# Neighbourhood attention cut into units of 16 grid columns by 8 rows with 32 key columns each, and values with both halves of V in one stationary operand

## The reference, cut to what matters

```
col_start = np.clip(qc - NA_WIN_COLS // 2, 0, GRID_W - NA_WIN_COLS)
col_mask = (qc[None, :] >= col_start[:, None]) & (qc[None, :] < col_start[:, None] + NA_WIN_COLS)
...
s_band = jnp.einsum('bqhd,brkhd->bhqrk', q_row, kb).astype(f32) * scale + bias.astype(f32)
s_band = jnp.where(col_mask, s_band, -jnp.inf)
s_ctx = jnp.einsum('bqhd,bchd->bhqc', q_row, k_c).astype(f32) * scale
s = jnp.concatenate([s_band.reshape(B, NA_HEADS, GRID_W, wr * GRID_W), s_ctx], axis=-1)
p = jax.nn.softmax(s, axis=-1).astype(v_c.dtype)
...
return (jnp.einsum('bhqrk,brkhd->bqhd', p_band, vb)
        + jnp.einsum('bhqc,bchd->bqhd', p_ctx, v_c))
```

## Time and profile before

| | us |
|---|---|
| median of 3 runs | 2733.66 |
| lowest, highest | 2729.28, 2734.5 |
| span of the profiled execution | 2731.3 |

### The profile page before, as it was taken

The page is one execution under the profiler, slowest core; times in us unless marked ns, Lnnn a source line. Parts: engine busy times, 40 slices in busy tenths (PEclk is TensorE's granted clock), DMA queues, the critical chain, the costliest instruction groups (busy, mean ns, idle before and its releaser), DMA issues.

```text
span 2731.3 us, 36972 instructions
## 1 busy us (share of the span) xinstructions
PE 2561.5 (94%) x14795; PEld 2194.1 (80%) x14795; DVE 1530.0 (56%) x2878; ACT 1096.8 (40%) x1928; POOL 321.7 (12%) x199
## 2 busy tenths in 40 slices
PE   7988889999997999998799999999899999899998
PEld 6877777878887877776688888889788887788887
DVE  3565556757757677777746443445555555633334
ACT  5455534222234655555521212113555565522223
POOL 2122100000012222221100000002222322000001
PEclk9999999999998999999899999999999999999999
DMA  4111033545531111111133333331322222132331
GB/s 112 47 47 47 24 96 124 166 139 166 166 116 47 32 39 39 39 33 45 48 105 122 103 118 105 116 113 46 72 54 59 62 61 60 62 106 79 105 98 61
DMA packets 247333, 223.86 MB, mean 82 GB/s; under 512 B 36916, under 2 KB 215898, under 8 KB 247162
## 3 DMA queue, kind: packets, MB, share of 16 engines
q1 hardware_dynamic: 247162, 221.49, 27.0%
HBM read 219.24 MB, written 2.22 MB: 81 GB/s over the span
## 4 chain that ended last, share of the span: by engine, by line
PE 78%; DVE 11%; ACT 7%; issue 4%; POOL 0%; DMA 0%; SPq 0%; DVEq 0%; POOLq 0%; ACTq 0%
PE ps L363 24%; PE ps L364 23%; PE ps L365 22%; DVE FR L527 2%; PE ps L2820 1%; PE ps L652 1%; ACT FR L522 1%; ACT whi L388 1%; PE ps L1071 1%; PE ps L2406 1%; ACT FA L2499 1%; PE ps L2831 1%; DVE hT L2579 1%; DVE FA L2619 1%; DVE raw L1444 1%
## 5 line engine op out<-in xcount | busy, mean ns | idle before, releaser
L363 PE MATMUL ps<-Uh,whi 128*128 128x512 f32 (+2 forms) x2544 | 904.8, 356 | 24.1 <-ACT FA L2518 5.9
L364 PE MATMUL ps<-Ul,whi 128*128 128x512 f32 (+2 forms) x2544 | 889.2, 350 | 0.0
L365 PE MATMUL ps<-Uh,wlo 128*128 128x512 f32 (+2 forms) x2544 | 887.7, 349 | 0.0
L363 PEld LDWEIGHTS ps<-Uh,whi 128*128 128x128 f32 x2544 | 491.7, 193 | 95.7 <-issue 20.0
L365 PEld LDWEIGHTS ps<-Uh,wlo 128*128 128x128 f32 x2544 | 490.4, 193 | 60.4
L364 PEld LDWEIGHTS ps<-Ul,whi 128*128 128x128 f32 x2544 | 491.5, 193 | 57.7
L388 ACT ACTIVATE whi<-raw 128x1024 fp32r<-128x1024 f32 (+2 forms) x205 | 296.4, 1446 | 539.0 <-PE ps L365 538.8
L399 DVE TENSOR_TENSOR wlo<-raw,whi 128x2048 fp32r<-128x2048 f32 (+2 forms) x121 | 248.2, 2052 | 299.1 <-ACT whi L388 299.0
L363 PE MATMUL ps<-FR,whi 128*128 128x512 f32 (+1 forms) x864 | 303.0, 351 | 7.3 <-DVE wlo L399 4.8
L364 PE MATMUL ps<-FR,whi 128*128 128x512 f32 (+1 forms) x864 | 300.0, 347 | 0.0
L365 PE MATMUL ps<-FR,wlo 128*128 128x512 f32 (+1 forms) x864 | 299.6, 347 | 0.0
(11 more groups left out here) (334 smaller groups left out, 3254.1 us busy)
## 6 DMA issues: line engine op xcount, KB each, us to landing
FA<-in_ada_w_dram SPq DMA_DIRECT2D x192, 256.0 KB, 2.8
raw<-in_ffn_w_gate_up_dram SPq DMA_DIRECT2D x44, 1024.0 KB, 5.1
raw<-in_ffn_w_down_dram SPq DMA_DIRECT2D x24, 768.0 KB, 4.4
raw<-in_w_in_dram SPq DMA_DIRECT2D x29, 512.0 KB, 3.9
raw<-in_da_wqkv_dram SPq DMA_DIRECT2D x24, 512.0 KB, 3.7
raw<-in_na_wqkv_dram SPq DMA_DIRECT2D x24, 512.0 KB, 3.8
raw<-in_w_ffn_gate_dram SPq DMA_DIRECT2D x11, 1024.0 KB, 5.3
raw<-in_w_ffn_up_dram SPq DMA_DIRECT2D x11, 1024.0 KB, 5.4
```

Source lines behind the costliest of these rows:

```text
L363: e.matmul(out, ah, bh, start=start, stop=False)
L364: e.matmul(out, ah, bl, start=False, stop=False)
L365: return e.matmul(out, al, bh, start=False, stop=stop)
```

## The change

A unit is now 16 grid columns by 8 rows (128 queries), and its near keys are 32 columns by 8 rows (256 keys) instead of all 512. The keys are stored with 8 columns of zeros ahead, so that unit `x` reads columns 16x to 16x+31 of each row, as a pattern of 2 x 8 x 16. The scores of a unit and head fill one bank of 512, the buffers `nP` are 512 wide, and a unit has four transposes. V is cut into 7 blocks (5 of near keys in strips of 16 columns shifted by 8, 2 of context). Its stationary operand of 128 columns holds, for a head, the high half beside the low half; a product with the high and one with the low half of the shares is then enough, 10 steps for a head and two units, and the two halves of the result stand in different partitions. ScalarE copies one (`low`), VectorE adds them (`full`), and then the sum is split (`o_hi`, `o_lo`) for both heads together. The table of a head is 128 by 256, loaded by 8 DMAs of 16 partitions and added to three masks. The two end pieces are strips of 32 grid columns (`Strip`) instead of halves of 256 tokens, also in the first gate tile of the feed-forward layer. The order of the steps, their costs and due times are new: the scores stand in twos, the transposes in twos.

```diff
+class Strip:
+    def __init__(self, c0):
+        self.seg, self.c0 = 0, c0
+    def of(self, t):
+        return t[:, 0:512].rearrange("p (r q) -> p r q", q=64)[:, :, self.c0:self.c0 + 32]
...
-ENDS = {"d": ("f1", (LEFT, RIGHT, CONTEXT)), "n": ("f2", (LEFT, RIGHT))}
+ENDS = {"d": ("f1", (LEFT, RIGHT, CONTEXT)), "n": ("f2", (Strip(0), Strip(32)))}
...
             for h in range(2):
-                K.hold(w, 2 * h, ("n_max", j, x, h))
-                K.hold(w, 2 * h + 1, ("n_max", j, x, h))
-            for a0, a1 in ((512, 768), (0, 512)):
+                K.hold(w, b0 + h, ("n_max", j, x, h))
+            for part in ("context", "near"):
                 for n, (q, k) in enumerate(((qh, kh), (qh, kl), (ql, kh))):
                     for h in range(2):
-                        t = e.matmul(K.ps[:, 1024 * h + a0:1024 * h + a1], q[r:r + 64, q0:q0 + P], k[r:r + 64, a0:a1],
-                                     start=n == 0, stop=n == 2)
+                            keys = k[r:r + 64, 16 * x:16 * x + 512].rearrange("p (r g c) -> p g r c", g=4, c=16)[:, 0:2, :, :]
+                            t = e.matmul(o[:, 0:256].rearrange("p (g r c) -> p g r c", g=2, c=16), queries, keys,
+                                         start=n == 0, stop=n == 2)
...
-            for y in range(6):
-                t = mm3(e, o[:, 0:256], vh[:, y, :], vl[:, y, :], th[:, y, :], tl[:, y, :], y == 0, y == 5)
+            order = ((2, 5, 0, 256), (3, 6, 0, 256), (1, 2 * p + 1, 0, 256), (0, 2 * p, 0, P), (4, 2 * p + 2, P, 256))
+            for z, (block, tile, c0, c1) in enumerate(order):
+                for m in range(2):
+                    t = e.matmul(o[:, c0:c1], vv[:, tile, P * h:P * h + P], K.nPT[h][m][:, block, c0:c1], start=z == 0 and m == 0,
+                                 stop=z == 4 and m == 1)
...
+        elif what == "low" and x % 2:
+            w.wait_ge(*K.at("n_values", j, x))
+            for h in range(2):
+                e.activation(K.nlow[r:r + 64, :], bank("o", j, p)[64 - r:128 - r, 256 * h:256 * h + 256], ACT.Copy).then_inc(*K.ev("n_copied", j, p, h))
...
+        elif what == "full" and x % 2:
+            w.wait_ge(*K.at("n_copied", j, p, 1))
+            for h in range(2):
+                e.tensor_tensor(full, o, low, ALU.add).then_inc(*K.ev("n_sum", j, p, h))
...
-                for half in range(2):
-                    rows = bass.AP(K.rpbd, ((2 * j + h) * 15 + 1 - half) * 128, [[1, 64], [128, 14], [1, 64]])
+                for r in range(8):
+                    rows = bass.AP(K.rpbd, ((2 * j + h) * 15 + r) * 128 + 40, [[1, 16], [128, 8], [1, 32]])
```

More of the change, by code:

```diff
@@ L61, in shape_constants @@
     c["levels"] = m.transpose(1, 0, 2).copy()
[L62 to L67, removed]
+    lane = np.arange(P) % 16
+    off = np.arange(32)
+    masks = []
+    for x in (0, 1, 3):
+        qcol = (16 * x + 15 - lane)[:, None]
+        kcol = (16 * x - 8 + off)[None, :]
+        first = np.clip(qcol - 8, 0, 48)
+        masks.append(np.where((kcol >= first) & (kcol < first + 16), 0.0, -1e30))
+    left, middle, right = masks
+    c["namask"] = np.concatenate([right[:, 0:24], left, middle], axis=1).astype(np.float32)
     return c
@@ L2689, in near_steps @@
             fill = k + q + [(0, ("table", j + 1, 0))] + v[0:2] + out[0:1] + v[2:3] + split + out[1:3] + v[3:] + out[3:]
+            spread = place(fill, NEAR_SHARE)
         else:
[L2691 to L2697 removed]
+            spread = [(split + out[0:1], []), (out[1:2], []), (out[2:4], []), ([], []), ([], []), ([], [])]
+            spread = [([s[1] for s in first], []) for first, _ in spread]
+        for p in range(2):
+            parts = [first + second for first, second in spread[3 * p:3 * p + 3]]
+            for h in range(2):
+                yield "turn", j, 4 * p + h
+            yield from parts[0]
+            for h in range(2):
+                yield "turn", j, 4 * p + 2 + h
+            yield from parts[1]
+            if p == 0 or j < 7:
+                for u in range(2):
+                    yield "scores", j + p, 2 * (1 - p) + u
+            else:
+                yield "out3", 7, 0
+            for h in range(2):
+                yield "values", j, 2 * p + h
+            yield from parts[2]
     yield "split_first", 7, "out"
@@ L2800, in near_tensor @@
             oh, ol = K.no[j % 2]
-            for h in range(2):
-                w.wait_ge(*K.at("n_o_lo", j, 6 + h))
+            w.wait_ge(*K.at("n_o_lo", j, 1))
             for n in (2 * x, 2 * x + 1):
@@ L2845 @@
                "v": (("v_out", 0.1),), "turn_v": (("tv_hi", 0.1),),
-               "scores": (("exp", 2.0), ("share", 5.0)), "turn": (("t_hi", 0.1),), "values": (("o_hi", 0.1),)}
+               "scores": (("exp", 1.0), ("share", 3.2)), "turn": (("t_hi", 0.1),), "values": (("low", 0.1), ("o_hi", 1.1))}
 def near_scalar(K, e, w):
```

280 lines of the change are left out of this document (167 added, 113 removed).

## The result

The changed kernel takes **2690.17 us** (median of 4 runs, 2684.62 to 2691.45) where the kernel before takes 2732.91 (4 runs, 2729.28 to 2734.5). The ratio of the two is 0.9843, with a 95% interval of 0.983 to 0.9855: 42.7 us less. The forecast was 2688.5, in a range of 2666 to 2712.

What follows compares the result with a forecast made beforehand. TensorE's queue was taken to bound the attention stage. Removed work of 57 us, partly offset by waits and a lower clock, takes the stage from 411 to 366 us: 2733.7 - 45 = 2688.5 us, range 2666 to 2712.

Steps and rivals of the forecast that it cites:

- Removed work: TensorE, per head pair: scores 1.6, transposes 1.65 and values 3.9 us less; 7.15 in sum, 57 over eight pairs.
- The new wait: Once a pair an `out` step waits 3.2 us for VectorE's sum; with VectorE's pace behind it, 4.2 us.
- The clock: After the wait TensorE runs at a lower clock: 1.5 us added to each pair.
- Pair 0: First head pair: 32.6 us of work, waits of 3.1 and 1.3, clock 1.5; 38.5 us instead of 46.2.
- Pair 1: Second head pair, holding one context projection more: 39.3 + 5.5 = 44.8 us.
- the tables' cover: Bias tables, sixteen small transfers at 0.42 us: the second head's is ready 3 us before VectorE wants it.
- Pair 7 and the end: Last head pair and stage end: 33.6 us of work and 16.4 of waits, 50 us instead of 64.4.
- (a): Rival: TensorE's waits don't grow, all 57 us and some 5 of old waits come: 2671.5 us; chance 0.23.
- (b): Rival: short runs in near keys and gate steps cost double, in part or whole: 2700 to 2712 us; chance 0.13.
- (d): Rival: slower than before, short runs at the plain fp32 step's rate, 92 us more: 2780 us; chance 0.03.
- (c): Rival: bias tables come late, 3.9 us in six pairs at 0.97 an issue: 2712 us; chance 0.06.
- (e): Rival: added stall twice the forecast, the gain in pairs 2 to 6 gone: 2710 us; chance 0.05.

Runs made afterwards that it cites:

- the early order: Changed kernel with ScalarE's copies and high part and VectorE's additions of a pair's values moved earlier in their queues: 2672.48 us.
- the keys in a row: Changed kernel with a unit's near keys read, and scores written, as 256 neighbouring columns instead of runs of 16: 2689.92 us.

## Why the prediction was right, point by point

- **Removed work.** Predicted 7.15 us a pair, 57 in all, and TensorE's busy time over the span fell by 56.7. The agreement of these two is luck, since the fall of the clock is in the second: in the early order, with the clock at 1.00 in pairs 2 to 6, it fell by 63.3, and by 8.1 in each of these pairs. With its changes of mode a pair had 40.8 us of work in the sum and has 41.4 at full clock. A unit of scores was put at 0.85 and takes 0.80; a head's values at 1.18 take 1.18, so the 128-column steps gain nothing, as said.
- **The new wait.** Predicted 3.2 us once in a pair, ended by VectorE's sum; measured 3.25 to 3.31. The sum counted 4.2, with 1.0 more for VectorE's pace behind it. No such idle time is in the trace (3.3 in all for a pair); whether the longer steps at the low clock hide it, no run shows. The exponentials stand 0.87 apart, not 0.92, because VectorE's maxima, 0.87 apart, pace them. What stands ahead of `low` was right row by row.
- **The clock.** Predicted 1.5 us a pair, 1.2 measured, at a mean clock of 0.95. Together: 0.6 more work, 0.9 less wait and 0.3 less for the clock make a pair of 45.84 for 46.5.
- **Pair 0**: 36.6 for 38.5. Its two waits are 2.2 and 0.7 us where I had 3.1 and 1.3, and the clock stays at 1.00, where I had 1.5 us for its fall. The work there was a little more than I counted.
- **Pair 1**: 46.7 for 44.8. The term that failed is the tables' cover. I worked it out for the steady pairs, where it held with more room than I gave it. In pair 0 the table of pair 1 is issued from 1966.8 on, only 6.8 us before the scores of pair 1, and there it was 2.6 us late. An issue was put at 0.42 us and took about 0.5.
- **Pair 7 and the end**: 56.0 for 50, the largest miss. The windows of before and after:

```profile
2284.20:2348.60 64.40, 52.47 (x345) 42.45 (x345) 48.33 (x118) 39.48 (x79) 9.21 (x8) 0.95 0.15 50
```
```profile
2249.50:2305.50 56.00, 40.26 (x246) 33.94 (x246) 43.98 (x109) 34.23 (x70) 9.22 (x8) 0.86 0.18 57
```

  TensorE's idle time grew from 11.9 to 15.7 us and the clock fell from 0.95 to 0.86, where the sum had all that is not work fall from 18.3 to 16.4. My sum counted the chain low, sum, high, low at 2.9 us for 1.7 and left out what stands in its way: ScalarE's split of a 2048-column chunk (1.89) and VectorE's (2.29), both now ahead of the copies and sums. The wait is 4.12 where 1.65 was. The last eight products behind it then run at the low clock, and from their start to the gate is 11.0 us in place of 8.7. The rest is that the two waits of pair 7 (3.28 and 2.70) were not all in my sum. These shares are read from the timelines; the edit on this place moved the split and met another wait, so it doesn't confirm them.

The total came within 1.7 us partly by luck, because the end's 6 us and pair 1's 1.9 too little stood against 5.2 us too much in pair 0 and pairs 2 to 6. Of the rivals, (a) did not come, but the early order shows that it was to be had: 2672.5, for the 2671.5 that it named, with TensorE idle for 172.8 us of the span as against 169.8 before. (b) and (d), the price of short runs, are ruled out by the gate steps of the trace and by the keys in a row. (c) came in one pair. (e) did not: 128-column steps save nothing, but the stall was as forecast and not twice as long.

## What to carry to other kernels

When work is taken from the busiest engine, ask for each buffer it reuses who frees it, and what stands ahead of the freeing instruction in that engine's queue: here a few short operations behind shares and a weight split cost 17.7 of the 60.4 us that there were to gain. A wait is seldom for one instruction: moving the copies and sums alone made the kernel slower, and moving the high part with them gave 17.7 us. A step added beside a wait that it fills costs little (8.6 of 37.9 us), and nearly its full time where the waits don't shrink (29.3), so judge removed work after the waits are mended: the same removal gave 42.7 us in one order and 60.4 in the other.

## What the runs showed of the hardware

- A wait can have a second price, the low clock behind it: with waits of 3.3 to 3.4 us in each pair the clock of pairs 2 to 6 is 0.93 to 0.96, with 2.9 it is 0.96 and 1.00 in turn, with 1.0 or less it is 1.00. Added work in the wait is partly paid back by it. The length of the wait alone does not decide it: with the same wait of 2.23 us in pair 0 the clock of that pair is 1.00 in the changed kernel and 0.95 in the early order. What does decide it stays open.
- A VectorE operation with two SBUF operands took 4.79 us instead of 0.48 beside a GpSimd operation of 4.50 us. So GpSimd is no free place for a split while VectorE works on such operands.
- Short runs cost TensorE nothing at 256 fp32 columns a step: six 64x256 steps take 0.35 us with the moving operand in runs of 16 columns and without, and gate steps that write eight runs of 32 columns into PSUM start 0.12 us apart, as contiguous ones do.
- A small transfer's issue takes 0.48 to 0.51 us on SyncE's queue when 16 or 32 stand in a row, for the 0.42 of a single one.
